# MLA attention on one core: P times V as three f32r products of hi and lo parts in place of one plain fp32 product

## The reference

```python
def causal_softmax_attention(q, k, v):
    ...
    def one(args):
        qi, bi = args
        t_idx = bi * Q_BLOCK + jnp.arange(Q_BLOCK)
        logits = jnp.einsum('bhqd,bhkd->bhqk', qi, k,
                            preferred_element_type=jnp.float32) * scale
        mask = s_idx[None, :] <= t_idx[:, None]
        w = jax.nn.softmax(jnp.where(mask, logits, -jnp.inf), axis=-1)
        return jnp.einsum('bhqk,bhkd->bhqd', w.astype(v.dtype), v)

def mla_layer(...):
    ...
    kv = (rmsnorm(c_kv, kv_norm_g) @ w_kv_up).reshape(B, S, N_HEADS, 2 * HEAD_DIM)
    k_nope, v = kv[..., :HEAD_DIM], kv[..., HEAD_DIM:]
    ...
    o = causal_softmax_attention(q.transpose(0, 2, 1, 3), k.transpose(0, 2, 1, 3),
                                 v.transpose(0, 2, 1, 3))
    o = o.transpose(0, 2, 1, 3).reshape(B, S, MIX_WIDTH) * jax.nn.silu(gate)
    return x + o @ w_out
```

## Time and profile before

| | |
|---|---|
| median of 3 runs | 1445.01 us (1440.18 to 1446.74) |
| the profiled execution, first to last instruction (span) | 1447.5 us |
| what lies around the span | no time of its own is given for the profiled execution, so its span stands for it; it is 2.5 us over the median |
| PE busy | 1407.9 us, 97% of the span |
| weight loads (PEld) | 1130.7 us, 78% |
| DVE busy | 766.3 us, 53% |
| ACT busy | 620.0 us, 43% |
| POOL busy | 261.0 us, 18% |
| mean granted clock of PE | 0.972 of full speed |

### The profile page before, as it was taken

One profiled execution on the slowest core, in us unless ns is written; L12 is line 12 of the kernel. 1 busy time (PEld: TensorE's weight loads), 2 busy tenths in 40 slices (PEclk: granted clock), 3 DMA queues, 4 the chain that ended last, 5 costly groups with the idle time before them and its releaser, 6 DMA issues.

```text
span 1447.5 us, 18393 instructions
## 1 busy us (share of the span) xinstructions
PE 1407.9 (97%) x6486; PEld 1130.7 (78%) x6486; DVE 766.3 (53%) x1271; ACT 620.0 (43%) x1100; POOL 261.0 (18%) x306
## 2 busy tenths in 40 slices
PE   6999999999999999999999999799999999999997
PEld 6888677788888877777888888688888888867776
DVE  5455788544732325666535536735764355256634
ACT  4347766343422335876235332123433333244434
POOL 3105733000000024441000004700000000423210
PEclk9999999999999998999999999899999999968899
DMA  4423000132232220001432332231333323300011
GB/s 151 131 60 122 16 0 0 59 102 88 87 102 97 93 92 24 0 0 29 146 102 88 118 101 88 73 98 53 101 101 109 97 80 101 102 14 0 1 44 58
DMA packets 54169, 106.10 MB, mean 73 GB/s; under 512 B 3460, under 2 KB 8280, under 8 KB 53720
## 3 DMA queue, kind: packets, MB, share of 16 engines
q1 hardware_dynamic: 52640, 98.91, 21.2%
q0 software_dynamic: 1376, 6.27, 1.4%
q10 hardware_dynamic: 88, 0.03, 0.0%
HBM read 103.11 MB, written 2.10 MB: 73 GB/s over the span
## 4 chain that ended last, share of the span: by engine, by line
PE 89%; DVE 4%; issue 4%; ACT 1%; DMA 0%; POOL 0%; POOLq 0%; SPq 0%; DVEq 0%; ACTq 0%
PE ps L421 21%; PE ps L423 21%; PE ps L422 21%; PE ps L569 3%; PE ps L816 2%; PE ps L701 2%; PE ps L798 2%; PE ps L593 2%; PE ps L691 2%; PE ps L692 2%; PE ps L676 1%; DVE w_lo L1379 1%; PE ps L582 1%; PE ps L799 1%; PE ps L677 1%
## 5 line engine op out<-in xcount | busy, mean ns | idle before, releaser
L1379 DVE TENSOR_TENSOR w_lo<-stage,w_hi 128x1024 fp32r<-128x1024 f32 (+4 forms) x188 | 239.3, 1273 | 489.2 <-ACT w_hi L906 489.1
L906 ACT ACTIVATE w_hi<-stage 128x1024 fp32r<-128x1024 f32 (+4 forms) x188 | 191.8, 1020 | 545.4 <-PE ps L423 545.4
L421 PE MATMUL ps<-a0h,w_hi 128*128 128x512 f32 x640 | 253.6, 396 | 9.4 <-DVE w_lo L1379 8.7
L422 PE MATMUL ps<-a0l,w_hi 128*128 128x512 f32 x640 | 251.4, 393 | 0.0
L423 PE MATMUL ps<-a0h,w_lo 128*128 128x512 f32 x640 | 251.2, 392 | 0.0
L421 PEld LDWEIGHTS ps<-a0h,w_hi 128*128 128x128 f32 x640 | 121.5, 190 | 37.2 <-DVE w_lo L1379 10.8
L423 PEld LDWEIGHTS ps<-a0h,w_lo 128*128 128x128 f32 x640 | 121.4, 190 | 25.6
L422 PEld LDWEIGHTS ps<-a0l,w_hi 128*128 128x128 f32 x640 | 121.4, 190 | 25.0 <-issue 0.2
L1906 POOL TENSOR_TENSOR small<-small 128x16 f32<-128x16 f32 (+2 forms) x15 | 33.4, 2226 | 535.7 <-DVE small L1457 396.2
L421 PE MATMUL ps<-w_hi,a0h 128*128 128x512 f32 (+1 forms) x320 | 122.2, 382 | 5.5 <-DVE w_lo L1379 5.5
L422 PE MATMUL ps<-w_lo,a0h 128*128 128x512 f32 (+1 forms) x320 | 120.5, 376 | 0.0
(11 more groups left out here) (271 smaller groups left out, 2572.0 us busy)
## 6 DMA issues: line engine op xcount, KB each, us to landing
stage<-in_a_w_in SPq DMA_DIRECT2D x48, 512.0 KB, 3.8
stage<-in_ple_w_gate SPq DMA_DIRECT2D x16, 512.0 KB, 3.3
stage<-in_w_kv_shared SPq DMA_DIRECT2D x16, 512.0 KB, 3.5
stage<-in_sb_w_in SPq DMA_DIRECT2D x16, 512.0 KB, 3.5
stage<-in_a_w_out SPq DMA_DIRECT2D x16, 512.0 KB, 3.3
stage<-in_b_w_in SPq DMA_DIRECT2D x16, 512.0 KB, 3.5
stage<-in_mla_w_in SPq DMA_DIRECT2D x8, 512.0 KB, 3.6
stage<-in_mla_w_out SPq DMA_DIRECT2D x8, 512.0 KB, 3.4
```

The costliest lines, as they stand in the source:

```text
L421: pe.matmul(bank, wh, mh, start=start, stop=False)
L422: pe.matmul(bank, wh, ml, start=False, stop=False)
L906: act.activation(w_hi[r % 2][:, 0:nk, 0:w], stage[r % 4][:, 0:nk, 0:w], ACT.Copy).then_inc(S("hi_ready"), 1)
L1379: dve.tensor_tensor(w_lo[r % 2][:, 0:nk, 0:w], stage[r % 4][:, 0:nk, 0:w], w_hi[r % 2][:, 0:nk, 0:w], ALU.subtract)\
```

## The change

`prT` becomes two tensors. `prT_h` is a copy from PSUM rounded to f32r, now made by ACT for all three banks in three pieces (512, 384, 384 columns); `prT_l` is what is left, made by DVE by subtracting each piece from the same bank, and each subtraction waits for ACT's piece. The values become `v_h`, rounded by ACT where it wrote `v_pair`, and `v_l`, made by POOL. P times V is then twelve f32r products in place of four plain fp32 ones. `prT_l` and `v_l` lie in the second weight slot (w_hi1, w_lo1), which stands unused during the heads; so the second piece of out0 can only be split once the last head's values are done, and DVE's gate of the last head is put ahead of that split.

```diff
+    for s in range(2):
+        RING = at[0]
+        w_hi.append(keep(f"w_hi{s}", [P, 2, T], F32R))
+        w_lo.append(keep(f"w_lo{s}", [P, 2, T], F32R))
...
-    prT = put("prT", [P, TRI], 5)
+    prT_h, prT_l = put("prT_h", [P, TRI], 5, F32R), put("prT_l", [P, TRI], 0, F32R, of=RING)
-    v_pair = put("v_pair", [P, MB, P], 18)
+    v_h = put("v_h", [P, MB, P], 18, F32R)
+    v_l = put("v_l", [P, MB, P], 6, F32R, of=RING)
...
         def mla_values(h, pair, first):
-            pe.wait_ge(S("pT_a"), h + 1)
-            pe.wait_ge(S("pT_b"), h + 1)
+            pe.wait_ge(S("pT_a"), 3 * h + 3)
             pe.wait_ge(S("v_ok"), pair + 1)
+            pe.wait_ge(S("v_lo"), pair + 1)
...
             for j in range(MB):
-                t = pe.matmul(ps[6][:, j * P:T], v_pair[:, j, :], prT[:, KEY_COL[j]:KEY_COL[j] + T - j * P],
-                              start=j == 0, stop=j == MB - 1, skip_group_check=True)
+                at = slice(KEY_COL[j], KEY_COL[j] + T - j * P)
+                if j == 0:
+                    pe.wait_ge(S("pT_b"), 3 * h + 3)
+                pe.matmul(ps[6][:, j * P:T], v_h[:, j, :], prT_h[:, at], start=j == 0, stop=False, skip_group_check=True)
+                pe.matmul(ps[6][:, j * P:T], v_l[:, j, :], prT_h[:, at], start=False, stop=False, skip_group_check=True)
+                t = pe.matmul(ps[6][:, j * P:T], v_h[:, j, :], prT_l[:, at], start=False, stop=j == MB - 1, skip_group_check=True)
...
-        pe.wait_ge(S("pT_a"), HEADS)
+        pe.wait_ge(S("pT_a"), 3 * HEADS)
+        pe.wait_ge(S("pT_b"), 3 * HEADS - 2)
         linear("out0", before=on_the_way(0))
...
-            act.activation(prT[:, 0:T], ps[3][:, :], ACT.Copy).then_inc(S("pT_a"), 1)
+            for b, (c, n) in enumerate(((0, T), (T, 384), (896, 384))):
+                act.activation(prT_h[:, c:c + n], ps[3 + b][:, 0:n], ACT.Copy).then_inc(S("pT_a"), 1)
...
+        act.wait_ge(S("o_done"), HEADS)
         split_to(lin["out0"].load0 + 1)
...
         def probs_T(h, first=False):
-            dve.wait_ge(S("pT_done"), h + 1)
             if not first:
                 dve.wait_ge(S("o_done"), h)
-            dve.tensor_copy(prT[:, T:T + 384], ps[4][:, 0:384])
-            dve.tensor_copy(prT[:, T + 384:TRI], ps[5][:, 0:384]).then_inc(S("pT_b"), 1)
+            for b, (c, n) in enumerate(((0, T), (T, 384), (896, 384))):
+                dve.wait_ge(S("pT_a"), 3 * h + (b + 1))
+                dve.tensor_tensor(prT_l[:, c:c + n], ps[3 + b][:, 0:n], prT_h[:, c:c + n], ALU.subtract).then_inc(S("pT_b"), 1)
...
+        o_gate(HEADS - 1, 1, PAIRS - 1, ps[6], "o_done", "o_read", "o_mla")
         split_to(lin["out0"].load0 + 1)
-        o_gate(HEADS - 1, 1, PAIRS - 1, ps[6], "o_done", "o_read", "o_mla")
...
+        def v_low(pair):
+            pool.wait_ge(S("v_ok"), pair + 1)
+            hs = slice(2 * pair, 2 * pair + 2) if isinstance(pair, int) else bass.ds(2 * pair, 2)
+            pool.tensor_tensor(v_l[:, :, :].rearrange("p m (a d) -> p m a d", a=2), kv_tok[:, :, hs, HD:2 * HD],
+                               v_h[:, :, :].rearrange("p m (a d) -> p m a d", a=2), ALU.subtract).then_inc(S("v_lo"), 1)
...
             for s in range(2):
+                if s:
+                    v_low(i - 1)
                 mla_head(2 * i + s, s)
```

More of the change, by code:

```diff
@@ L134, in build @@
     stage = [keep(f"stage{s}", [P, 2, T]) for s in range(4)]
-    w_hi = [keep(f"w_hi{s}", [P, 2, T], F32R) for s in range(2)]
-    w_lo = [keep(f"w_lo{s}", [P, 2, T], F32R) for s in range(2)]
+    w_hi, w_lo = [], []
+    for s in range(2):
+        RING = at[0]
+        w_hi.append(keep(f"w_hi{s}", [P, 2, T], F32R))
+        w_lo.append(keep(f"w_lo{s}", [P, 2, T], F32R))
     SG = at[0]
@@ L351, in build @@
     LOOPED = ("g_g",)
+    assert lin["out0"].load0 % 2 == 0
+    v_l = put("v_l", [P, MB, P], 6, F32R, of=RING)
     def result_bank(m, half):
@@ L575, in mla_probs_T @@
             if not first:
-                pe.wait_ge(S("pT_a"), h)
-                pe.wait_ge(S("pT_b"), h)
+                pe.wait_ge(S("pT_a"), 3 * h)
+                pe.wait_ge(S("pT_b"), 3 * h)
             for n, q in enumerate(reversed(range(MB))):
@@ L1112, in mla_pair @@
             hs = slice(2 * i, 2 * i + 2) if isinstance(i, int) else bass.ds(2 * i, 2)
-            act.activation(v_pair[:, :, :].rearrange("p m (a d) -> p m a d", a=2), kv_tok[:, :, hs, HD:2 * HD], ACT.Copy)\
+            act.activation(v_h[:, :, :].rearrange("p m (a d) -> p m a d", a=2), kv_tok[:, :, hs, HD:2 * HD], ACT.Copy)\
                .then_inc(S("v_ok"), 1)
@@ L1968, in _ @@
         for s in range(2):
+            if s:
+                v_low(0)
             mla_head(2 + s, s)
@@ L1975, in _ @@
             for s in range(2):
+                if s:
+                    v_low(i - 1)
                 mla_head(2 * i + s, s)
         link.end(PAIRS - 2)
+        v_low(PAIRS - 1)
         root(nrm, MB, "nrm_in", 2, "nrm_ok")
```

## The result

The changed kernel takes 1458.89 us (median of 4 runs, 1456.70 to 1460.64); the kernel before, run beside it, 1443.05 (1440.18 to 1446.74). The ratio is 1.0097, with a 95% interval of 1.0066 to 1.0128: 15.8 us slower by the medians, 9.5 to 18.5 by the interval. The forecast was 1457.0, slower, in a range from 1450 to 1466.

What follows compares the result with a forecast made beforehand. It took PE as never idle but DVE's way from transposes to maxima as equally tight. 7.5 + 4.9 + 0.8 - 0.3 - 0.8 gave +12.1 us: 1459.6 profiled, 1457 as a median, range 1450 to 1466.

Steps and rivals of the forecast that it cites:

- VectorE's way sets the pace: MLA heads: DVE's longer way from the transposes to the next head's maxima sets the pace; slower, 74 in 100.
- First half +0.94: First head of a pair: waiting for ACT's piece and one more DVE piece delay the first maximum 0.94 us.
- Second half +0.70: Other head of a pair: maxima 0.76 us later, less 0.06 counted back for waits inside the maxima.
- Slack of 0.05 a head: Between DVE's chain and PE at the head's transposes: 15 x 0.05 = 0.8 us taken off the sum.
- The products, 1.85 us: P times V on PE: twelve f32r products take 1.85 us a head, 0.31 less, hidden behind DVE's way.
- PE's new standing time: PE idle before the probabilities' transposes, released by DVE's pr, some 2.3 us a pair.
- The late pieces: POOL's v_l, ready by 201.7 before 202.6, and the second weight slot's late split, covered by 0.4 us: no cost.
- The end +0.8: Start of out0: it waits for ACT's three pieces and DVE's first subtraction, 0.8 us later.
- The clock was a rival: Heads: PE's pauses lower the clock, up to 8 us more, 1460 to 1466; 8 in 100.
- The sum for the heads: All heads: eight of the first kind give 7.5 us, seven of the second 4.9, less 0.8 of slack.
- the -0.3 of the last values: Last head's values, which lie on PE's way: 0.3 us saved by the new products.
- the sum +12.1: Whole kernel: head terms, end and slack together, 12.1 us slower, 1459.6 on the profiled execution.

Runs made afterwards that it cites:

- Experiment 2: Changed kernel's copies, subtractions, waits and buffer places, but the four old plain fp32 products; stretch 119.07 us against the changed kernel's 119.01, single runs 1448.94 to 1462.06.
- experiment 4: Changed kernel with ScalarE copying the 384-column pieces first and VectorE's 512-column subtraction left out; 5.2 us over the kernel before (2.5 to 7.8).
- Experiment 1: Kernel before with its values as three f32r products of equal operands, copies and order unchanged; 0.4 to 5.6 us faster than before.
- experiment 3: Kernel before with one more 384-column PSUM copy on VectorE per head, ahead of the next maxima; median 3.3 us above before.
- experiment 9: Changed kernel with prT_l and v_l in memory of their own, so the second weight slot is split before the last values; 1460.70 us.
- experiment 5: Changed kernel with VectorE's three subtractions spread among the next head's maxima and the lo products last on TensorE; 1451.73 us, run again 1452.05.
- 10: Changed kernel with subtractions spread among the maxima, lo products last, and fewer, joined reciprocals on VectorE; 1456.15 us, run again 1452.80.
- e9_again: Second run of the kernel with spread subtractions and fewer, joined reciprocals, its profile at the lower clock among the first heads; 1452.80 us.

## Why the prediction was right, point by point

**VectorE's way sets the pace: right, and shown.** Experiment 2 has the whole loss without the new products; experiment 4 takes four fifths of it away with one subtraction and a shorter first piece on ACT.

**First half +0.94: right.** Measured +0.95 to the first maximum, and nothing behind it, except in three heads, where 0.24 was lost beside POOL's copy, which the prediction had not. Piece by piece too: from the first subtraction (205.24) to the maximum (206.78) it is 1.54 us, the 0.60 + 0.47 + 0.47 that were taken.

**Second half +0.70: mis-sized.** To the first maximum it is +0.75, as worked out (0.76). But the half grew only from 7.19 to 7.55, +0.36: behind the maximum 0.39 came back, where I had counted 0.06. The traces tell where: DVE had waited for TensorE there (experiments 1 and 3), and the maxima, the gap between the first two (1.32 before, 1.14 now) and a normalising of 128 columns beside POOL's copy (0.46 in the earlier trace rows, 0.29 in all heads now) each waited a little, which no longer happens when all comes later. That PE's order and DVE's chain end together was true of both halves, and I took it as true of the ways there; a tie at the end doesn't say that both were tight all along.

**Slack of 0.05 a head: wrong in one half.** It is none in the first and about 0.4 in the second (experiment 3).

**The products, 1.85 us: 1.96.** Experiment 1 gives 0.20 saved per head in place of 0.31; in the changed kernel the first product of a head is followed after 0.32 (200.26 to 200.58), not 0.23. It lay on no path, as said: experiment 2.

**PE's new standing time: right in kind, wrong in place and size.** Forecast were 2.3 us a pair before the transposes, released by DVE's pr; it is 1.2 us a pair ahead of the key's transposes, released by ACT's qT, and less besides. ACT's qT stands behind two of its exponentials, and these wait for the maxima, so the pause still comes from DVE's way.

**The late pieces were covered, as predicted.** POOL made v_l in 1.28 us, less than the 1.53 to 1.83 assumed, and nobody waited for it. PE has no wait at the second weight slot either (experiment 9).

**The end +0.8: right, with a follow-up that wasn't there.** out0's first product waited 1.53 where it had waited 0.69: +0.84. The fall of the clock behind it, 1.5 us, was not in the sum. The clock was a rival, but placed inside the heads, where it stayed at 1.00 although PE stood 1.2 us and more a pair.

**The sum for the heads: near, and partly by luck.** The stretch grew by 11.9 us. The terms of the sum that lie in it make 12.4; the -0.3 of the last values lies behind it. But the eight first halves grew by 8.1, not 7.5, the seven second halves by 3.1, not 4.9, and the 0.8 of slack that was taken off did not show. Terms that were off by 0.6 to 1.8 us in both directions cancel.

**The time.** The medians say +15.8 (9.5 to 18.5), the sum +12.1. The traces have 11.9 in the stretch, 0.8 of which is the end, and 1.5 at out0's start: 13.4. Runs at a like clock come near it: at a mean granted clock of 0.974 three runs of the changed kernel have a mean of 1459.5, and 19 of the kernel before, from the experiments, 1446.0; that is 13.4 as well, though a like clock leaves out what the fall at out0's start costs. What is beyond isn't resolved by medians of four runs each. The forecast stood on 1445.0 for the kernel before, and the median beside it was 1443.05: that shift brings 1458.9 nearer to 1457 than 15.8 is to 12.1.

**No version beats the kernel before.** Against it the best with the full result, 5 and 10, are 0.5% slower. The loss can be halved by order, but the work on VectorE stays.

## What to carry to other kernels

Splitting an operand into hi and lo parts saves on TensorE, but its price is paid where the parts are made: a copy that two engines shared becomes a chain of two engines, with one piece more on the second. Before counting a saving, mark one event per head, and measure for each half of the period how far behind it each engine's next step starts and whether it waited; a single period can have two different bounds. Work moved to GpSimd isn't free for VectorE either: ask what VectorE runs at that moment, and place GpSimd's long pieces beside steps that read PSUM. And where medians of near kernels disagree with their traces, compare runs at the same mean clock.

## What the runs showed of the hardware that was not expected

- A GpSimd tensor_tensor of 1.28 us held up two kinds of VectorE operation on SBUF until it ended: a scalar_tensor_tensor of one column took 1.07 us in place of 0.15, a tensor_scalar of 512 columns 1.32 in place of 0.49. A reciprocal of one column beside it took its usual 0.15, subtractions of 384 columns from PSUM their usual 0.55. Which of two that meet waits turned on less than 0.01 us between their starts: 0.59 or 0.35 for the same piece of VectorE.
- Twelve f32r products in a row (three each of 512, 384, 256 and 128 columns) take 1.96 us from the first start to the start of what follows; four plain fp32 products of the same columns take 2.16.
- Of eight profiles in which PE stood 1.53 us ahead of out0, seven have TensorE's clock at 1.2 GHz around its start; so have both with 1.91 us of standing, and the one with 1.45 and the three with 0.69 have not. The kernel of experiment 5 has one profile of each kind. Inside the heads, with waits of up to 1.2 us, the clock stayed at 1.00 in all but one profile (e9_again).
- Runs with a lower mean granted clock take longer, by about 5 us for 0.003: the kernel before, in 19, 16, 20 and 9 runs at 0.974, 0.975, 0.976 and 0.977, has means of 1446.0, 1444.6, 1443.6 and 1440.8 us.
